# Two fp32 blocks on one core: softmax, convolution and time steps of the first block in another order

## What is computed

```python
h = rmsnorm(x, pre_mix_norm[l])
proj = h @ w_in[l]
z, xbc, dt_raw, q, k, v, gates = split_cols(proj, IN_SPLITS)
...
xbc = jax.nn.silu(depthwise_conv(xbc, conv_w, conv_b))
dt = jax.nn.softplus(dt_raw + dt_bias)
a_dt = dt * a;  a_cs = jnp.cumsum(a_dt, axis=-1)
...
logits = jnp.einsum('bnqgrd,bnkgd->bngrqk', qb, kb) * (ATTN_HEAD_DIM ** -0.5)
logits = jnp.where(valid, logits + bias, -jnp.inf)
m = jnp.maximum(jnp.max(logits, axis=-1, keepdims=True), sink_l)
p = jnp.exp(logits - m)
p = p / (jnp.sum(p, axis=-1, keepdims=True) + jnp.exp(sink_l - m))
out = jnp.einsum('bngrqk,bnkgd->bnqgrd', p, vb)
```

## Time and profile before

| | before |
|---|---|
| median of 3 runs | 980.12 us (978.96 to 980.62) |
| the profiled execution's own time | 980.26 us |
| its span, first to last instruction | 978.5 us |
| busy TensorE / VectorE / ScalarE / GpSimd | 96% / 65% / 53% / 7% |
| chain of work that ended last | TensorE 80%, VectorE 12%, ScalarE 6%, DMA 1% |

### The profile page before, as it was taken

The page is one execution under the profiler, slowest core; times in us unless marked ns, Lnnn a source line. Parts: engine busy times, 40 slices in busy tenths (PEclk is TensorE's granted clock), DMA queues, the critical chain, the costliest instruction groups (busy, mean ns, idle before and its releaser), DMA issues.

```text
span 978.5 us, 13876 instructions
## 1 busy us (share of the span) xinstructions
PE 943.4 (96%) x5798; PEld 834.9 (85%) x5798; DVE 634.6 (65%) x787; ACT 519.2 (53%) x662; POOL 65.5 (7%) x74
## 2 busy tenths in 40 slices
PE   6999999999999999989999999899999999999998
PEld 5988889877788888879998887789888889998887
DVE  5398988987678664766665443977664766655443
ACT  7447996676654643365554334465564355554331
POOL 0001110121110000000000000800000000000000
PEclk9999999999999999989999999899999999999999
DMA  7933323452225376435555555854345445555541
GB/s 280 354 113 114 130 87 130 172 194 86 87 86 194 129 284 226 178 112 189 179 192 191 179 209 172 204 193 160 133 156 188 168 167 198 197 176 176 211 171 44
DMA packets 24974, 166.55 MB, mean 170 GB/s; under 512 B 2938, under 2 KB 3066, under 8 KB 6224
## 3 DMA queue, kind: packets, MB, share of 16 engines
q1 hardware_dynamic: 22320, 156.12, 45.2%
q0 software_dynamic: 2592, 9.54, 3.3%
HBM read 164.57 MB, written 1.08 MB: 169 GB/s over the span
## 4 chain that ended last, share of the span: by engine, by line
PE 80%; DVE 12%; ACT 6%; issue 1%; DMA 1%; SPq 0%; ACTq 0%; DVEq 0%
PE ps L351 66%; PE ps L380 4%; DVE w_lo L1163 4%; ACT w_hi L835 2%; DVE conv_acc L1353 2%; PE ps L616 1%; PE ps L560 1%; PE ps L545 1%; PE ps L666 1%; PE ps L420 1%; PE ps L638 1%; DMA raw<-in_w_stream 1%; PE ps L625 1%; PE ps L640 1%; DVE gates L1445 1%
## 5 line engine op out<-in xcount | busy, mean ns | idle before, releaser
L1163 DVE TENSOR_TENSOR w_lo<-raw,w_hi 128x2048 fp32r<-128x2048 f32 x147 | 337.9, 2304 | 219.4 <-ACT w_hi L835 219.4
L835 ACT ACTIVATE w_hi<-raw 128x2048 fp32r<-128x2048 f32 x147 | 279.8, 1906 | 238.0 <-PE ps L351 231.6
L351 PE MATMUL ps<-ht_hi,w_hi 128*128 128x256 f32 x856 | 244.5, 286 | 0.0
L351 PE MATMUL ps<-ht_lo,w_hi 128*128 128x256 f32 x856 | 242.9, 284 | 0.0
L351 PE MATMUL ps<-ht_hi,w_lo 128*128 128x256 f32 x856 | 242.8, 284 | 0.0
L351 PEld LDWEIGHTS ps<-ht_hi,w_hi 128*128 128x128 f32 x856 | 164.5, 192 | 1.4 <-issue 1.3
L351 PEld LDWEIGHTS ps<-ht_hi,w_lo 128*128 128x128 f32 x856 | 164.6, 192 | 0.0
L351 PEld LDWEIGHTS ps<-ht_lo,w_hi 128*128 128x128 f32 x856 | 164.5, 192 | 0.0
L351 PE MATMUL ps<-w_hi,ht_hi 128*128 128x512 f32 (+1 forms) x288 | 112.8, 392 | 0.7 <-DVE w_lo L1163 0.7
L351 PE MATMUL ps<-w_hi,ht_lo 128*128 128x512 f32 (+1 forms) x288 | 110.6, 384 | 0.0
L351 PE MATMUL ps<-w_lo,ht_hi 128*128 128x512 f32 (+1 forms) x288 | 110.5, 384 | 0.0
(11 more groups left out here) (263 smaller groups left out, 1204.0 us busy)
## 6 DMA issues: line engine op xcount, KB each, us to landing
raw<-in_w_stream SPq DMA_DIRECT2D x146, 1024.0 KB, 4.9
bias<-rel_scratch POOLq DMA_DIRECT2D x1, 3072.0 KB, 17.4
bias<-in_rpb POOLq DMA_DIRECT2D x16, 128.0 KB, 4.4
gates<-in_gate_bias POOLq DMA_DIRECT2D x2, 768.0 KB, 5.7
x_first<-in_x_in SPq DMA_DIRECT2D x2, 512.0 KB, 4.1
x<-in_x_in POOLq DMA_DIRECT2D x1, 1024.0 KB, 7.2
g_post<-in_post POOLq DMA_DIRECT2D x2, 512.0 KB, 10.3
out_y<-x SPq DMA_DIRECT2D x4, 256.0 KB, 2.0
```

The source lines that it names most:

```text
L351: ins = pe.matmul(o, still, moving, start=first and n == 0, stop=last and n == 2, skip_group_check=True)
L835: act.activation(w_hi[s % SPLIT_RING][:, 0:width(s)], raw[s % RAW_RING][:, 0:width(s)], ACT.Copy).then_inc(hi_ready, 1)
L1163: dve.tensor_tensor(w_lo[s % SPLIT_RING][:, 0:width(s)], raw[s % RAW_RING][:, 0:width(s)], w_hi[s % SPLIT_RING][:, 0:width(s)].bitcast(F32 ...
```

## The change

Six edits: (1) the dt piece moves from slot 4 to slot 2, amid q, and with it `dt_exp`, `softplus` and `minus_log_dt` by two slots; (2) the scale of the logits moves into ScalarE's copy of q, and bias, store and maximum become one instruction per head, `tensor_tensor_reduce`, that starts from the sink; (3) TensorE does `values1` and `conv_turn` between the two halves of the slot's stream in place of after it; (4) ScalarE's SiLU comes ahead of `split_hi`, the exponentials ahead of `values_hi`; (5) VectorE's softmax comes ahead of `split_lo` of the next slot (the same place in its list but for the sums of slot 10), and `conv_taps` ahead of `values_lo` and of the copy of the turned chunk; (6) the eight table instructions L1417 move to ScalarE's slot 19, behind SiLU, `split_hi` and the copy.

```diff
-S_DT = 4
+S_DT = 2
...
-    ("q", S_Q, "feat", 4), ("dt", S_DT, "dt", 1), ("kv", S_KV, "kv", 2), ("xbc", S_XBC, "feat", 16),
+    ("q", S_Q, "feat", 2), ("dt", S_DT, "dt", 1), ("q", S_DT + 1, "feat", 2), ("kv", S_KV, "kv", 2), ("xbc", S_XBC, "feat", 16),
...
-            def ssd_between(s):
-
+            def slot_middle(s):
+
+                if 0 <= s - 10 < 8:
+                    values1(s - 10)
+                if s >= 11 and (s - 11) % 2 == 0 and (s - 11) // 2 < 6:
+                    conv_turn((s - 11) // 2)
...
-                if 0 <= s - 10 < 8:
-                    values1(s - 10)
                 if 0 <= s - 9 < 8:
                     prob_turn("a1", s - 9, 0, logit1)
-
-                if s >= 11 and (s - 11) % 2 == 0 and (s - 11) // 2 < 6:
-                    conv_turn((s - 11) // 2)
...
             for s in range(SLOTS):
+                name, form, chunk, part, opens, closes = slots[s]
+                if s >= 11 and (s - 11) % 2 == 0 and (s - 11) // 2 < 8:
+                    c = (s - 11) // 2
+                    act.wait_ge(conv_tapped, 4 * (c + 1))
+                    if c == 4:
+                        ready(act, ("a1o", 7))
+                    dest = conv_acc[c % 2][:, :, :] if c < 4 else bc[:, 4 * (c - 4):4 * (c - 4) + 4, :]
+                    act.activation(dest, conv_acc[c % 2][:, :, :], ACT.Silu).then_inc(conv_silu, 1)
                 if s + AHEAD < SLOTS:
                     split_hi(s + AHEAD)
...
-                                       ACT.Copy).then_inc(*drain_of(("q", chunk, half)))
+                                       ACT.Copy, scale=HD ** -0.5).then_inc(*drain_of(("q", chunk, half)))
...
+                if s == 19:
+                    act.wait_ge(cum_ready, 1)
+                    for c in range(RT):
+                        for j in range(PER_GROUP):
+                            ins = act.activation(cum_l[c][:, :, j, :], cum[:, 2 * c:2 * c + 2, :], ACT.Identity,
+                                                 scale=quad[:, 2 + j:3 + j], bias=quad[:, 6 + j:7 + j])
+                    ins.then_inc(tables_ready, 1)
...
+            def softmax_sink(a):
+
+                k, r, u = a % 2, a // 4, a % 4
+                sink, at0 = param("sink"), P * (1 - r)
+                if a == 0:
+                    dve.wait_ge(bias1_landed, 16)
+                if a >= 2:
+                    ready(dve, ("a1p", a - 2, 1))
+                for e in range(2):
+                    key = ("a1s", a, e)
+                    ready(dve, key)
+                    for h in range(2):
+                        i, head = 2 * e + h, 8 * (u // 2) + 2 * (u % 2) + 4 * e + h
+                        ins = dve.tensor_tensor_reduce(logit1[k][:, i, :], ps[:, 4 + e, h * TOK:h * TOK + TOK],
+                                                       bias1[:, head, at0:at0 + TOK], 1.0,
+                                                       sink[:, 4 * u + i:4 * u + i + 1], ALU.add, ALU.max,
+                                                       soft[:, k, 0, i:i + 1])
+                    ins.then_inc(*drain_of(key))
...
+                if 0 <= s - 8 < 8:
+                    softmax_sink(s - 8)
                 late = s in (S_WO - 1, S_MI - 1, S_Q2 - 1, S_WO2 - 1, S_MI2 - 1)
                 if s + AHEAD < SLOTS and not late:
                     split_lo(s + AHEAD)
...
+                if s >= 9 and (s - 9) % 2 == 0 and (s - 9) // 2 < 8:
+                    conv_taps((s - 9) // 2, (0, 1))
+                if s >= 10 and (s - 10) % 2 == 0 and (s - 10) // 2 < 8:
+                    conv_taps((s - 10) // 2, (2, 3))
                 if 0 <= s - 10 < 8:
                     values_lo(s - 10)
```

More of the change, by code:

```diff
@@ L124, in slot_table @@
         assert first == len(table)
+        before = sum(row[0] == name for row in table)
         for i in range(count):
@@ L130, in slot_table @@
             else:
-                table.append((name, form, i // 2, i % 2, i % 2 == 0, i % 2 == 1))
+                table.append((name, form, (before + i) // 2, i % 2, i % 2 == 0, i % 2 == 1))
     assert len(table) == SLOTS
@@ L699, in _ @@
                     pe.wait_ge(co_ready, 1)
-                stream(s, ssd_between)
+                stream(s, slot_middle)
                 if s == 0:
@@ L939, in _ @@
             for s in range(SLOTS):
+                name, form, chunk, part, opens, closes = slots[s]
[6 more added lines that the diff above has]
+                    act.activation(dest, conv_acc[c % 2][:, :, :], ACT.Silu).then_inc(conv_silu, 1)
                 if s + AHEAD < SLOTS:
                     split_hi(s + AHEAD)
-                name, form, chunk, part, opens, closes = slots[s]
                 if s == 0:
@@ L964, in _ @@
                     act.activation(dtw[:, 2], dtw[:, 1], ACT.Exp).then_inc(dt_exp, 1)
[L965 to L972, removed]
+                if 0 <= s - 8 < 8:
+                    exps(s - 8, logit1, 0, True)
+                if 0 <= s - 10 < 8:
                     values_hi(s - 10)
@@ L1255, in add_residual, with softmax_max @@
                         ins.then_inc(*drain_of((name, n, r)))
-            def softmax_max(name, a, logit, bias, sink):
+            def softmax_sink(a):
[15 more added lines that the diff above has]
+                    ins.then_inc(*drain_of(key))
+                emptied(dve, ("a1s", a, 0)), emptied(dve, ("a1s", a, 1))
+                link(dve.tensor_scalar(soft[:, k, 1, :], soft[:, k, 0, :], -1.0, None, ALU.mult))
+                dve.tensor_tensor(soft[:, k, 2, :], soft[:, k, 1, :], sink[:, 4 * u:4 * u + 4],
+                                  ALU.add).then_inc(negmax_ready, 1)
+            def softmax_max(name, a, logit, bias):
                 k = a % 2
@@ L1412, in decay_tables @@
                 emptied(dve, "cum")
-                link(dve.scalar_tensor_tensor(cum[:, :, :], cum_lo[:, :, :], quad[:, 1:2], cum_sign[:, :, :],
-                                              ALU.mult, ALU.add))
-                for c in range(RT):
-                    for j in range(PER_GROUP):
-                        ins = dve.tensor_scalar(cum_l[c][:, :, j, :], cum[:, 2 * c:2 * c + 2, :],
-                                                quad[:, 2 + j:3 + j], quad[:, 6 + j:7 + j], ALU.mult, ALU.add)
-                ins.then_inc(tables_ready, 1)
+                dve.scalar_tensor_tensor(cum[:, :, :], cum_lo[:, :, :], quad[:, 1:2], cum_sign[:, :, :],
+                                         ALU.mult, ALU.add).then_inc(cum_ready, 1)
             def feed_forward(name, c):
@@ L1493, in _ @@
                     dve.tensor_copy(dest, ps[:, 5, :]).then_inc(*drain_of(("turn", c, 1)))
-                if s >= 9 and (s - 9) % 2 == 0 and (s - 9) // 2 < 8:
-                    conv_taps((s - 9) // 2, (0, 1))
-                if s >= 10 and (s - 10) % 2 == 0 and (s - 10) // 2 < 8:
-                    conv_taps((s - 10) // 2, (2, 3))
                 if 0 <= s - 8 < 8:
                     softmax_divide(s - 8, logit1, 0, True)
-                if 0 <= s - 7 < 8:
-                    a = s - 7
-                    r, u = a // 4, a % 4
-                    head = 8 * (u // 2) + 2 * (u % 2)
-                    if a == 0:
-                        dve.wait_ge(bias1_landed, 16)
-                    at0 = P * (1 - r)
-                    softmax_max("a1", a, logit1,
-                                lambda e: bias1[:, head + 4 * e:head + 4 * e + 2, at0:at0 + TOK],
-                                neg_sink[:, 4 * u:4 * u + 4])
                 if s == 10:
@@ L1630, in _ @@
                     softmax_max("a2", a, logit2,
-                                lambda half: bias2[:, r, 4 * g + half:4 * g + half + 3:2, :], None)
+                                lambda half: bias2[:, r, 4 * g + half:4 * g + half + 3:2, :])
                 if 0 <= s - 95 < 4:
```

19 lines of the change are left out of this document (3 added, 16 removed).

## The result

The changed kernel takes 1002.79 us (median of 4 runs, 999.24 to 1005.06) against 979.54 us before: the ratio is 1.0224, with a 95% interval of 1.0205 to 1.0242. It is slower by 22 us by this ratio (the medians are 23 apart). The forecast was 997 us within 986 to 1004.

The account below looks back on a forecast made before the run. TensorE was taken to set the time in slots 7 to 25, with VectorE at 89%. 980.26 us plus 11.6 for the chain through the eighth SiLU and 5.1 for clock falls gave 997.0, forecast 997, range 986 to 1004.

Parts of the forecast that it names:

- Step 1: dt piece two slots earlier: slot 7 starts 1.9 us late, at 54.4; slot 9 at 68.2; the clock's fall goes, -1.7.
- T10: Start of the last matmul of slot 10 on TensorE: 84.11 us before, forecast 83.3.
- Step 2: Slots 11 to 18: SiLU (2.2) and taps (3.2) join each pair's chain, 22.6 us for a full pair; +8.3 us by slot 18.
- T: Start of the last matmul of an even slot; the chain was to let `scores` begin 14.5 us after it.
- pairs of 22 to 23: Sign on TensorE: time between last matmuls of successive even slots becomes 22 to 23 us.
- Step 3: Slots 19 to 25: ScalarE and VectorE no longer overlap; eighth SiLU at 217.2 against 205.60, +11.6 us, never given back.
- the sum without falls: Case with no clock falls counted: eighth SiLU starts at 217.2 us.
- Step 4: VectorE's fused bias, store and maximum: 1.8 us for four heads, 0.8 less than before; moves the sum by 0.
- Step 5: `values1` and `conv_turn` in mid-piece on TensorE: same matmuls, `ot_lo` and `xtok` still behind `w_lo` and taps; 0.
- Step 6: TensorE's granted clock falls after the idle of each of four pairs, 1.7 us each; three counted, +5.1 us.
- same chain, clock stays: Rival: the chain lengthens as forecast but TensorE's clock does not fall; 991.7 us, chance 0.22.
- faster: Rival: SiLU fills ScalarE's time before `piece_done`, starting before T + 1.5, and TensorE's waits go; 971 us, chance 0.07.

Follow-up runs that it names:

- a_taps: Changed kernel with VectorE's eight taps put back behind `values_lo` and the copy of the turned chunk: ratio 1.0067 to the kernel before.
- a_fill: Changed kernel with idle turns of the identity added on TensorE in the four long waits of slots 11, 13, 15 and 17: ratio 1.0136.
- a_silu: Changed kernel with ScalarE's SiLU put back behind `split_hi`: ratio 1.0079 to the kernel before.
- a_three: Changed kernel with taps put back behind `values_lo` and the copy, exponentials behind `values_hi` and the copy of the turned chunk: ratio 1.0005.
- b_silutaps: Kernel before with only SiLU moved ahead of `split_hi` and taps ahead of `values_lo` and the copy: ratio 1.0253.
- a_turn: Changed kernel with only `conv_turn` put back behind the slot, `values1` staying in mid-piece: ratio 1.0230 to the kernel before.
- b_mid: Kernel before with only `values1` and `conv_turn` moved between the halves of the slot's stream: ratio 1.0108.
- a_both: Changed kernel with SiLU put back behind `split_hi` and taps behind `values_lo` and the copy: ratio 1.0094 to the kernel before.
- b_ttr: Kernel before with only the scale in the copy of q and bias, store and maximum fused into one instruction per head: ratio 0.9974.
- best1: Changed kernel with SiLU, exponentials, taps, `conv_turn` and tables put back; early dt, fused instruction, earlier softmax and mid-piece `values1` stay: ratio 0.9958 to the kernel before.

## Why the prediction held, and where it did not

The direction, the mechanism and the range were right; the point of 997 was 5.8 us low, because the low clock was counted too small.

*Step 1, dt.* Slot 7 at 54.43, forecast 54.4; slot 9 at 68.44, forecast 68.2; no low clock behind either. That the first agrees to 0.03 us is partly luck: a_taps, a_fill and a_silu, which are the changed kernel up to there, reach slot 7 at 54.59, 56.13 and 56.82. In slot 0 of the last two, matmuls start 0.21 us apart from 13.7 us to 17.5 and to 19.0, where they are 0.12 apart in the others. So times counted from the start of two profiles compare only to within 2.4 us; the lengths between two points of one profile, used below, don't have this error. T10 came at 84.06, forecast 83.3: 0.8 low. `values1` costs slot 10 rather 1.1 than 0.9, as its 1.08 record shows; the rest is spread over slots 7 to 10.

*Step 2, the chain.* T + 14.6 to `scores`, forecast 14.5. The four pairs, 25.67, 24.50, 22.71 and 24.26 us, less the clock's 3.0, 1.6, 1.6 and 2.6, are 22.7, 22.9, 21.1 and 21.7; forecast 22.6, 22.6, 20.8 and 22.0. This term, 8.3 us, was right to 0.4. The pairs of 22 to 23 that the forecast names as a sign hold only with the clock's share taken off. That SiLU and taps both are links is shown by a_silu and a_three, and that they suffice by b_silutaps. What the step left out is a second branch of nearly equal length: table load, exponentials, `ot_hi`, `ot_lo`. It cost nothing in the change, being shorter than the taps, and cost 6 us, low clock included, once these were gone (a_taps against a_three).

*Step 3, slots 19 to 25.* From the fifth SiLU at 184.47 to the eighth at 227.71 is 43.2 us, forecast 42.6. The 0.6 lies between the sixth and the seventh, 14.90 where the step had 14.3 (its terms add up to 14.4), and it goes with the fifth fall: in a_fill, which has that fall, the same distance is 14.82, in a_taps and a_three, whose clock stays at 1.00 in slot 21, 14.36 and 14.34. Edit 6, the tables, was not tried by itself. The eighth is 10.5 later than the 217.2 of the sum without falls.

*Step 4, the fused instruction.* What stands as `ISA` in the VectorE list of the change reads so in the timeline:

```profile
86.88 0.48 DVE L1273 CUSTOM_DVE_ANT_0 logit<-ps,bias,params 128x256 f32<-128x256 f32 x1
87.29 0.08 DVE L1273 DVE_READ_ACCUMULATOR2_ANT soft<- 128x1 f32 x1
87.29 0.48 DVE L1273 CUSTOM_DVE_ANT_0 logit<-ps,bias,params 128x256 f32<-128x256 f32 x1
```

It starts every 0.41 us, 1.65 for four heads, where I took 1.8, and the row that stores the maximum (0.08) lies beside the next one. The Trainium skill's "VectorE: DVE Perf Modes" (section on the TRN2 errata), by which four were about 1.6 as an estimate, agrees with the trace. In the forecast it changed nothing, and in the changed kernel VectorE waits 3.45 us for `w_hi` right behind it. Alone it wins 2.5, in the profiled execution mostly by the clock, which step 4 didn't ask about.

*Step 5, mid-piece turns.* For `conv_turn` the cost of 0 was right in this change (a_turn); `values1` was not put back by itself. Its reason was thin: the cover is the early SiLU, and without it the price is a wait of 1.8 to 3.0 us in each of six slots (b_mid, a_both).

*Step 6, the clock.* This is the term of the sum that was mis-sized. I took three falls of 1.7, 5.1 us. There were five in the stretch. The four of slots 11 to 17 counted in full, since none lay where TensorE would have waited anyhow, and they cost 1.6 to 3.0 each: 8.8 by the windows, 8.3 by a_fill. That is 3.7 of the 5.8 us. The fifth, 1.6 by its window, was in step 3's 0.6, since SiLU and not TensorE sets the time there (TensorE waits 1.01 us for the eighth); T10's 0.8, this 0.6 and the pairs' 0.4 make most of the rest. So both halves of the term were low: the number of falls that count, and the price of one, which came from a single case. The rival *same chain, clock stays* (991.7) is near what a_fill came to, 994.5 with one fall left in slot 21.

The rival *faster* needed a SiLU before T + 1.5. It began at T + 3.9 (table load at 87.92), behind `prob_out`, as argued against it.

## What to carry to other kernels

In a strict list, what is moved ahead of a step that all engines pass (here the split of the next weights) is paid in full by every round in which the chain through it is the longest, however idle its engine looks in the totals (in a_three, where that chain was short again, the same SiLU cost nothing): ScalarE was busy for 71% of the stretch and VectorE got 12% less work, and the kernel lost 2.2%. Price such a change as a ring: from the end of one round, through each engine's list, to the end of the next, both branches of it; and a zero that rests on another edit is a zero only with that edit. Then add what TensorE's clock takes after each new wait, here 8 of 22 us.

## What was not expected of the hardware

The length of a wait alone does not tell whether the clock falls behind it. It fell behind 1.67 us and 2.01, and it stayed at 1.00 behind 2.10 in b_ttr (above) and behind 3.00 in a_silu at 174:

```profile
174.00:176.00 2.00, 1.43 (x13) 1.43 (x14) 2.00 (x2) 1.25 (x3) 0.00 (x0) 1.00 0.00 0
176.00:178.00 2.00, 2.00 (x19) 2.00 (x18) 2.00 (x6) 2.00 (x5) 0.00 (x0) 1.00 0.59 106
```

It fell behind every wait of 3.2 us and more between slots 11 and 17 of the changed kernel. What a fall costs varies too, from 1.6 to 3.0 us of TensorE's time, though the waits of 3.91 and 3.93 us ahead of them were alike. And in a part that no kernel here touches, behind the wait of 1.59 us named at best1, it cost 2.6 us before, 1.3 in best1, and in a_silu nothing, behind the same 1.59:

```profile
433.00:443.00 10.00, 7.01 (x49) 5.61 (x48) 9.12 (x23) 6.13 (x17) 0.00 (x0) 1.00 0.00 0
```

What decides it was not tried and stays open; for a forecast it means a range per fall, and not the one price seen before.
